# Hybrid sparse/window attention block: index keys split from the product's banks, two tiles run together at the head of each half, setup moved into the last projection tiles

## What is computed

```python
proj = jnp.einsum('bld,dc->blc', x, w_in)
qa, ka, va, ga, qi, ki, wi, qb, kb, vb, gb = jnp.split(proj, offsets, axis=-1)
# group A: indexer, top-k, attention over the chosen keys (8 heads, 1 shared k/v head)
dots  = jnp.einsum('bqhd,bsd->bqhs', qi_blk, ki)               # 4 index heads
score = jnp.einsum('bqh,bqhs->bqs', w_blk * idx_scale, jax.nn.relu(dots))
_, idx = lax.top_k(jnp.where(visible, score, -inf), 256)
# group B: window of two 64-token chunks, sinks, 8 query heads on 2 k/v heads
y = jnp.concatenate([ya * jax.nn.silu(ga), yb * jax.nn.silu(gb)], -1) @ w_out
x = layer_norm(ALPHA * x + y, ln_g, ln_b)
```

## Time and profile before

| | |
|---|---|
| three runs | 1780.77, 1780.04, 1773.29 us; median 1780.04 |
| profiled execution | 1779.32 us, its span 1777.5 us, granted clock 0.915 |
| PE busy | 1493.7 us (84%) |
| DVE busy | 1222.7 us (69%) |
| ACT busy | 913.0 us (51%) |
| POOL busy | 423.9 us (24%) |

### The profile page before, as it was taken

How to read it: one execution, slowest core, us unless ns; L and a number is a source line. 1 busy time by engine, 2 the same in 40 slices (tenths; PEclk the granted TensorE clock), 3 DMA queues, 4 the chain that set the end, 5 groups by cost and what they waited for, 6 DMA issues and landing times.

```text
span 1777.5 us, 18604 instructions
## 1 busy us (share of the span) xinstructions
PE 1493.7 (84%) x6470; PEld 1080.3 (61%) x6520; DVE 1222.7 (69%) x2001; ACT 913.0 (51%) x1766; POOL 423.9 (24%) x270
## 2 busy tenths in 40 slices
PE   7998988899799174676776878889999899998997
PEld 5886766788678153544554545545554555557886
DVE  3379899779899967556658676786559734106776
ACT  3385947559568655554652446756555344430000
POOL 3323325532223321111113111101110302122221
PEclk9999989999999676677876999999999899999999
DMA  6321223312222731222222122112211302115442
GB/s 209 96 83 66 95 85 127 129 60 95 60 86 72 156 73 26 56 56 52 57 58 66 31 53 49 36 37 61 62 38 25 88 5 91 53 49 172 142 142 95
DMA packets 104782, 137.37 MB, mean 77 GB/s; under 512 B 6594, under 2 KB 81222, under 8 KB 104558
## 3 DMA queue, kind: packets, MB, share of 16 engines
q1 hardware_dynamic: 91504, 93.16, 19.5%
q10 hardware_dynamic: 9536, 32.25, 4.7%
q0 software_dynamic: 3648, 10.76, 2.3%
HBM read 93.81 MB, written 42.34 MB: 77 GB/s over the span
## 4 chain that ended last, share of the span: by engine, by line
PE 52%; DVE 23%; ACT 13%; issue 7%; DMA 3%; POOL 2%; SPq 0%; ACTq 0%; DVEq 0%; POOLq 0%
PE psum L979 13%; PE psum L1133 9%; PE psum L1182 9%; ACT above L836 6%; DVE above L1277 5%; PE psum L1111 2%; DVE junk L1361 2%; DVE score L1226 2%; PE psum L1112 2%; PE psum L1098 2%; PE psum L1066 2%; DVE score L1299 2%; PE psum L1097 2%; PE psum L1110 2%; ACT accept L842 2%
## 5 line engine op out<-in xcount | busy, mean ns | idle before, releaser
L1277 DVE TENSOR_SCALAR_CACHE_REDUCE above<-dist,trial 128x512 bf16<-128x512 int32 (+13 forms) x224 | 346.1, 1545 | 6.1
L1133 PE MATMUL psum<-prob,vw 128*65 128x512 f32 x544 | 291.8, 620 | 56.5 <-ACT prob L930 56.5
L836 ACT ACTIVATE above<-dist,trial 128x384 bf16<-128x384 int32 (+13 forms) x224 | 280.7, 1253 | 69.6 <-DVE trial L1258 33.8
L930 ACT ACTIVATE prob<-psum 128x512 f32<-128x512 f32 x272 | 159.7, 594 | 301.9 <-PE psum L1112 289.0
L979 PE MATMUL psum<-x_hi,w_hi 128*128 128x512 f32 x640 | 252.0, 394 | 24.3 <-DVE x_lo L1313 11.6
L979 PE MATMUL psum<-x_lo,w_hi 128*128 128x512 f32 x640 | 250.3, 391 | 0.0
L979 PE MATMUL psum<-x_hi,w_lo 128*128 128x512 f32 x640 | 250.2, 391 | 0.0
L1361 DVE CUSTOM_DVE_ANT_0 junk<-psum,mask 128x1024 bf16<-128x1024 f32 (+7 forms) x192 | 171.1, 912 | 61.7 <-PE psum L1066 31.2
L1066 PE MATMUL psum<-ka_ext,qa_ext 128*128 128x512 f32 (+3 forms) x320 | 143.9, 526 | 65.3 <-DVE part_max L1361 55.4
L1111 PE MATMUL psum<-qa_mix,ka_mix 128*128 128x512 f32 x272 | 165.6, 609 | 0.0
L1066 PEld LDWEIGHTS psum<-ka_ext,qa_ext 128*128 128x128 f32 x320 | 60.2, 200 | 153.3 <-DVE part_max L1361 98.5
(11 more groups left out here) (159 smaller groups left out, 2963.7 us busy)
## 6 DMA issues: line engine op xcount, KB each, us to landing
raw<-w_tiles SPq DMA_DIRECT2D x40, 512.0 KB, 3.7
proj<-staged ACTq DMA_DIRECT2D x40, 512.0 KB, 2.7
qa_raw<-proj SPq DMA_DIRECT2D x34, 256.0 KB, 4.8
qb_raw<-proj SPq DMA_DIRECT2D x34, 256.0 KB, 4.2
yt_raw<-y_t SPq DMA_DIRECT2D x16, 512.0 KB, 5.3
x_row<-x_res SPq DMA_DIRECT2D x16, 512.0 KB, 4.0
out<-z ACTq DMA_DIRECT2D x16, 512.0 KB, 2.6
x_raw<-xT SPq DMA_DIRECT2D x12, 512.0 KB, 4.8
```

Of the source, the lines that this page charges most:

```text
L836: nc.scalar.activation(above[:, 0, 0:n], src, ACT.Sign, scale=-1.0, bias=u, accum_out=count[:, 0:1]).then_inc(sign_counted, 1)
L930: nc.scalar.activation(prob[:, unit % 3, :], psum[:, 4 + unit % 2, :], ACT.Exp, scale=0.125).then_inc(a_prob, 1)
L1133: pe.matmul(psum[0:65, 6 + g, :], vw[:, kt, 0:65], prob[:, u % 3, :], start=(kt == 0), stop=(kt == b)).then_inc(a_used, 1)
L1277: v.tensor_scalar(above[:, 1, 0:n], src, u, None, ALU.is_ge, ALU.add, accum_out=count[:, 1:2]).then_inc(own_counted, 1)
```

## The change

It does five things.

1. **Index keys from PSUM.** Tile 2 of a half holds `ki` in its first 64 rows. ACT now copies it from banks 0 and 1 twice into `ki_hi`, DVE subtracts twice into `ki_lo`; the load from DRAM, the staging tile and POOL's subtraction are gone. Tile 4, which reuses the banks, waits for `ki_lo_ok`.
2. **Two tiles k by k.** Tiles 0 and 1 of each half share the loop over k, the second one three steps behind.
3. **Planner.** `index1` to `index5` are 62, 122, 196, 320, 428 (before 60.738, 123.678, 197.394, 308.652, 414.0), `queries` stands 8 ahead of `dots` instead of 3.6, norms 8 and 9 follow tile (1, 1) instead of (1, 2), and the chunks of pair 4 with keys of the second half come last.
4. **Transition in the last tiles.** The keys `ka` are loaded, rounded and split during the search of pair 5, and so are `power`, `load_qb(0)`, `round_qb(0)` and `split_qb(0)`. The waits at the end are spread to where each thing is used.
5. **Layout.** The SBUF tiles of the attention part stand in another order, so that those loaded early lie over storage that is free by then.

```diff
-PROJ = {'start': 6.547, 'index1': 60.738, 'index2': 123.678, 'index3': 197.394, 'index4': 308.652, 'index5': 414.0, ...
+PROJ = {'ask': 8, 'lead': 3, 'lag_low': 3.2, 'keys_a': 463.0, 'start': 6.547, 'index1': 62, 'index2': 122, 'index3': 196, 'index4': 320, 'index5': 428, ...
...
-               (1, 2): (8, 9), (1, 4): (10, 11), (1, 6): (12, 13), (1, 8): (14, 15)}
+               (1, 1): (8, 9), (1, 4): (10, 11), (1, 6): (12, 13), (1, 8): (14, 15)}
...
+    chunks = [(j, c, min(512, n - c)) for j in range(2) for c in range(0, n, 512)]
+    return sorted(chunks, key=lambda chunk: p == NPAIR // 2 and chunk[1] >= HALF)
...
-    for place in tiles:
-        work += [(0.68, ("product", *place, i)) for i in range(2 * KT)]
+    for half, t in tiles:
+        place = (half, t)
+        if t == 0:
+            lead = int(PROJ["lead"])
+            for k in range(KT + lead):
+                for u, step in ((0, k), (1, k - lead)):
+                    if 0 <= step < KT:
+                        work += [(0.68, ("product", half, u, 2 * step + m)) for m in range(2)]
+        elif t >= 2:
+            work += [(0.68, ("product", *place, i)) for i in range(2 * KT)]
...
-        put(time - 3.6, "queries", p)
+        put(time - PROJ["ask"], "queries", p)
...
+    ready = PROJ["keys_a"]
+    put(ready, "load_keys_a")
+    for i in range(2):
+        put(ready + 6.0 + 8.0 * i, "round_keys_a", i)
+        put(ready + 6.5 + 8.0 * i, "split_keys_a", i)
+    put(end[(1, N_TILES - 3)] + 5.0, "power")
+    put(end[(1, N_TILES - 3)] + 5.0, "load_qb", 0)
+    put(end[(1, N_TILES - 2)] + 1.5, "round_qb", 0)
+    put(end[(1, N_TILES - 2)] + 2.0, "split_qb", 0)
...
             def round_keys(half):
-                act.wait_ge(ki_in, 32 * (half + 1))
-                copy(ki_hi[:, half * HALF:(half + 1) * HALF], ki_raw[:, :]).then_inc(ki_hi_ok, 1)
+                act.wait_ge(tile_mm, half * N_TILES + 3)
+                keys = psum[0:HD, 0:2, :].rearrange("p b n -> p (b n)")
+                copy(ki_hi[0:HD, half * HALF:(half + 1) * HALF], keys)
+                copy(ki_hi[HD:P, half * HALF:(half + 1) * HALF], keys).then_inc(ki_hi_ok, 1)
...
+            def split_keys(half):
+                dve.wait_ge(ki_hi_ok, half + 1)
+                dve.wait_ge(tile_out, half * N_TILES + 3)
...
+            def load_keys_a():
+                sp.wait_ge(stored[0], 16 * (N_TILES // 2 + 2))
+                sp.wait_ge(summed, 4 * chunks_before(NPAIR - 2))
...
+            def round_keys_a(i):
                 ks = slice(HALF * i, HALF * (i + 1))
-                act.wait_ge(stage_in[i], 32)
+                act.wait_ge(keys_in, 32)
+                act.wait_ge(norm_mm, NB)
+                copy(ka_ext[0:HD, 0, ks], keys_a_raw[0:HD, ks]).then_inc(keys_hi, 1)
+                copy(ka_ext[0:HD, 1, ks], keys_a_raw[0:HD, ks])
+                copy(ka_mix[HD:P, ks], keys_a_raw[HD:P, ks]).then_inc(keys_taken, 1)
...
                     wait_if(pe, tile_out, g - 1)
+                    if t == 4:
+                        pe.wait_ge(ki_lo_ok, half + 1)
```

More of the change, by code:

```diff
@@ L384, in hybrid_kernel @@
         mask_out = sem("mask_out")
[L386 removed]
+        sel_in = sem("sel_in")
         keys_taken = sem("keys_taken")
@@ L488, in n_dots_to @@
         def n_dots_to(p, j, c, h):
-            return 2 * (chunks_before(p) + j * len(chunks(p)) + c // 512) + h // 2
+            place = [chunk[0:2] for chunk in index_chunks(p)].index((j, c))
+            return 2 * (chunks_before(p) + place) + h // 2
         def wait_if(engine, s, value):
```

223 lines of the change are left out of this document (120 added, 103 removed).

## The result

| | kernel before | changed kernel |
|---|---|---|
| median of 16 runs each, taken in turns | 1775.4 us | 1785.0 us |
| range of these runs | 1767.1 to 1788.5 | 1777.7 to 1797.2 |
| ratio, 95% interval | | 1.0049 (1.0028 to 1.0069) |
| profiled execution, its span | 1779.3, 1777.5 | 1794.1, 1792.3 |
| a second series (e13, 9 runs; 14 of before) | 1777.6 us | 1786.7 us, ratio 1.0064 (1.0031 to 1.0097) |

The changed kernel is slower by some 9 us, not by 22.8 (9.6 and 9.1 between the medians of the two series; by the ratios 5 to 12 and 6 to 17). The profiled execution is one of the long ones of its series; against the profile of before it is 14.8 us longer.

A forecast was written before the change was run, and what follows sets the result against it. It took a nearly solid DVE and ACT chain of 258.6 us from pair 4's first sum, its start set by PE, as the bound. Terms summed to +22.8 us on 1779.3 or 1780.0: forecast 1803, range 1787 to 1812.

The forecast's parts named there:

- First half: Up to tile (1, 1)'s weights: 2 us later, bounds 1.6 earlier and 4 later.
- Head of the second half and pair 4's place: Before pair 4's first sum: 8 products +5.5, half clock +2.4, later place of dots +11.5, norm 10's copies +0.9 us.
- Norm 11: Between pair 4's first and second pair of heads: the norm and its copies leave DVE idle, +3.0 us.
- Pair 4's search: An evacuation's 1.3 us wait for PE at the search's end goes: -1.3 us, bounds -1.3 and 0.
- Pair 4's masks and pair 5's sums: The stretch between pair 4's and pair 5's searches; the prediction's sum had no term for it.
- Pair 5's search: Key copies make ACT late by step 16, +3, and query rounding adds +1.5: +4.5 us, bounds 0 and 7.6.
- Rival A: In pair 5's search, key rests hold DVE for their whole length: +5.3 us over the term, 1808; chance 0.12.
- Transition: Before window block 0: DVE's 5.69 us wait for window logits goes, -5.7 us, bounds -5.7 and -3.
- Behind pair 6: Everything after pair 6's first sum; the prediction's sum had no term for it.
- Rival B: At the second half's head, (1, 1)'s weights are ready by step 3 and products fill waits: 1789.5 us; chance 0.12.
- C: PE reaches pair 4's first dots by the time DVE is free, closing the 7.2 us hole: 1770 us; chance 0.10.

The follow-up runs named there:

- e13: The changed kernel run and profiled again, unaltered; 1786.7 us, ratio to the kernel before 1.0064.
- e5: The changed kernel with index queries asked for 3.6 instead of 8 before a pair's dots; ratio to the kernel before 1.0084.
- e4: e1 with the first half's tiles 0 and 1 in sequence too; 54.9 us from tile (1, 1)'s start to pair 4's first sum, total not given.
- e3: The changed kernel with the second half's tiles 0 and 1 in sequence and pair 4's dots at 308.652 instead of 320 in the table; 1770.9 us.
- e12: The changed kernel with norms 10 and 11 behind tile (1, 5) instead of (1, 4); median the same as the changed kernel's.
- e11: e10 with the attention keys' copies and rests behind pair 5's search, beside its masks; pair 6's first sum 1.5 us later than e10's, total not given.
- e10: e3 with pair 4's dots at 298 and pair 6's query load ahead of pair 5's mask stores; block 0's bias to pair 6 20.2 us, total not given.
- e1: The changed kernel with the second half's tiles 0 and 1 one after the other again; ratio to the kernel before 0.9986.
- e14: e10 with pair 5's dots at 417 instead of 428 and the attention keys' load at 452 instead of 463 in the table; 1754.8 us.
- e7: e3 with six repeats of one DVE instruction ahead of pair 4's search, as a delay; 1780.0 us.
- e8: e3 with eleven repeats of one DVE instruction ahead of pair 4's search, as a delay; 1783.7 us.

## Why the prediction was wrong, point by point

The sum, term by term, against the marks of the first profile and of e13. The last column names the run that measured the term by itself.

```
term                                             said    marks    e13    by itself
first half, to the weights of (1, 1)             +2.0    -4.0    -3.3   e5: 2.8 of the error
head, clock, pair 4's place, norm-10 copies     +20.3   +20.1   +19.3   head 7.6 (e4), place 12.4 (e3)
norm 11 between heads                            +3.0    +5.0    +3.4   e12: 5.8, or 4.2 from e13
pair 4's search                                  -1.3    -0.7    -0.7
pair 4's masks and pair 5's sums                  0      -0.2    +0.2   masks +2.7, sums -2.9
pair 5's search                                  +4.5    +4.7    +4.6   e11: 3.5 of it
pair 5's masks, to block 0's bias                -5.7    -9.3    -9.3   e11: 3.4 of it
block 0's bias to pair 6                          0      +0.9    +0.7   e10: 0.7
sum at pair 6                                   +22.8   +16.4   +14.9
behind pair 6                                     0      -1.6    -7.8   medians: some -6
```

**First half: failed, 6 us.** I put the border at +2, with 1.6 earlier as the lowest bound. The step that failed is "Pair 1's search has the query rounding inside (+1.0)": I counted what the early rounding adds and not what it takes away where it was, DVE's scans beside GpSimd's rests. It came 4.0 earlier, outside both bounds. e5 shows this for 2.8 us of the 6; for the rest, in pair 1's search, the cause is open.

**Head of the second half and pair 4's place: right, with one row misread.** From the start of (1, 1)'s weights to pair 4's first sum I added 20.3, and it is 62.5 - 42.5 = 20.1. The wait, its releaser and the half clock behind it are as forecast; only it is 17 and not 12, since I took step 4's row for step 3's (306.86 for 302.93). The length of the wait is no term of the sum, so this cost nothing. The 8 products and the clock come out at 7.6 for 7.9, and the place at 12.4 for 12.4. All five profiles with the long wait have the half clock behind it, but e1 and e14 have it without one, so the long wait is not the only thing that brings it.

**Norm 11: size, +5.0 for +3.0, and +3.4 in e13.** The gap was 6.1 us in the first profile: the 24 matmuls of the norm took 4.54 instead of 2.67 us, at a granted clock of 0.66 from 379 to 384. In e13, e1, e4 and e5 it was 4.5 us; the dots and ACT's relu behind the norm, some 2 us, I had left out.

**Pair 4's search: the number was right by luck.** It is -0.7 for -1.3, but not by the term that I gave. The kernel before had one of GpSimd's weight rests (382.39 to 387.25) beside its order step, the changed kernel has none there, and that is worth -2.8 to the search's first compare:

```profile
381.44 3.54 DVE L1245 TENSOR_TENSOR score<-score,dist 128x2560 int32<-128x2560 int32 x1
385.02 3.58 DVE L1246 TENSOR_SCALAR dist<-score 128x2560 int32<-128x2560 int32 x1
```
```profile
402.49 2.83 DVE L1292 TENSOR_TENSOR score<-score,dist 128x2560 int32<-128x2560 int32 x1
405.35 1.50 DVE L1293 TENSOR_SCALAR dist<-score 128x2560 int32<-128x2560 int32 x1
```

Against it DVE now waits 2.75 us for ACT at step 16, where it waited for nothing before; its wait behind the search fell from 4.9 to 2.5.

**Pair 4's masks and pair 5's sums: put at nothing, and two errors that cancel.** In the kernel before GpSimd splits a tile's weights beside pair 5's sums (491.3 to 495.6), in the changed kernel beside pair 4's masks (492.9 to 500.4): the sums are 2.9 shorter and the masks 2.7 longer.

**Pair 5's search: right** to 0.2. Rival A had the right engine pair and the wrong place: the key rests took 2.40 us in the search and held nobody there.

**Transition: failed, 3.6 us.** The step that failed is "So DVE's 5.69 us wait goes: -5.7", as all that the transition gains. The wait did go, and what came late next cost 0.9, as the bounds allowed; but the stretch became 9.3 shorter. What I missed is again the port: of a step that moves I priced the place where it goes and not the one it leaves, 3.9 us of masks.

**Behind pair 6: not in the sum.** I took the rest as fixed. It is fixed in work, but its length differs by some 20 us from run to run of one kernel, and the changed kernel's runs lie some 6 us lower. Why they do is open. Without this the medians would differ by 15 to 16.

So of the 13 us between +22.8 and +9.6, 6.4 by the first profile (7.9 by e13) are terms of the sum, and the others lie in a part that the sum didn't have. Rival B (the second head fills its wait) and C (pair 4 not late) did not occur; the change was slower for the reasons given, by less.

## What to carry to other kernels

Where a step is moved, price the place it leaves as carefully as the place it goes to: in both terms that I got wrong by over 2 us a good part of what I missed was there (2.8 and 3.9 us). Look for any long DVE instruction with a GpSimd row beside it, and take both records apart; a table of start times is worth tuning by which of these meet. And compare two kernels by a mark at the end of the part that was changed, not by the total alone, when the total has a tail whose length varies from run to run. Take the mark from more than one profile: two of the same kernel differed by up to 1.7 us here, and a conclusion that e1's profile alone suggested did not outlast the others.

## What the runs showed of the hardware

**The tail's length comes in steps.** The sixteen profiles agree within 0.6 us at block 2's bias, all but one (74.4 to 75.0 us behind mark 6, one 70.5), and then spread: block 6's bias stands 252 to 266 us behind the mark, in three groups (252 to 254, 258 to 260, 265 to 266), and from there to the end all need 864 to 868. The spread goes with TensorE's clock: from block 2's bias to block 6's the profiles take 178 to 192 us, with 64 to 94 us of it at the half level, and the long ones have more of it (correlation 0.96). The clock stands at 1.00 or 0.50 (2.4 or 1.2 GHz) in short turns there, and not in the same places in each run. The same place of block 3, 15 us behind its bias, in e7 and in e8:

```profile
784.00:789.00 5.00, 3.15 (x10) 2.10 (x9) 4.86 (x13) 1.72 (x8) 0.00 (x0) 0.73 0.00 0
```
```profile
793.00:798.00 5.00, 3.30 (x12) 1.56 (x11) 4.86 (x11) 2.21 (x11) 0.00 (x0) 1.00 0.00 0
```

The changed kernel shows it against itself: blocks 3 to 6 took 139.1 us in its first profile and 132.6 in e13. Its longer runs have the lower mean clock (1777.7 us at 0.918, 1797.2 at 0.905). What picks the pattern was not tried.

**One engine's record holds the other's work.** A GpSimd rest of 2.4 us showed as 4.8, a DVE step of 2.8 as 4.9, in pairs that meet, and both fit within 0.3 us with each waiting for the other's end. Busy time of either is then no measure of its work.
